# Up rows of the PEER stage: DVE adds them one rank at a time for 128 tokens, in place of PE; low parts shared anew between DVE and POOL

## The chip, the cores and the metric

One Trainium2 chip, one core. The metric is the device time of one execution in microseconds (us), the median of the runs of a kernel. Engines: PE (TensorE, matrix products), DVE (VectorE), ACT (ScalarE), POOL (GpSimd), SP (SyncE, which issues most DMAs). SBUF is the on-chip memory, PSUM the banks that PE writes.

## The reference

A two-layer decoder trunk on 512 tokens of width 1024, fp32. Layer 0 is attention, layer 1 a gated MLP; after each comes `peer_layer`, which this change touches:

```
q  = (xb @ w_query)                  # 8 heads x 2 halves x 128
s1, i1 = top_k(scores half 0, 16);  s2, i2 = top_k(scores half 1, 16)
top, ci = top_k(s1 + s2 pairs, 16)   # 16 of 128 * 128 experts for each head
idx = e1 * 128 + e2;  g = softmax(top)
hid = gelu(einsum('td,thkd->thk', xb, expert_down[idx]))
y   = einsum('thk,thkd->td', g * hid, expert_up[idx])
```

So each token reads 8 heads x 16 = 128 ranks: 128 rows of `expert_down` and 128 of `expert_up`, 1024 fp32 (4 KB) each.

## The kernel before

**Two ways for two groups of tokens.** For 384 tokens (`TD`) the kernel goes through all 16384 experts densely: down stage (128 tiles) and up stage (128 tiles) multiply whole weight tiles with dense hidden values and gates. For the first 128 tokens (`G`) it fetches only the chosen rows by indirect DMA. The up half of this second way is what changes.

**Weight tiles.** A tile is 128x1024 fp32, 512 KB. SP loads it into a ring of 4 (`raw`, L208); ACT makes its high part (`split_hi`, L215); POOL or DVE subtracts to get the low part (`split_lo`, L221); PE multiplies (`columns_step`, L246): 8 chunks of 3 matmuls, high x high, high x low, low x high (L254 to L256), 384 columns. High and low parts have rings of 3, and both are made `AHEAD` = 2 tiles early. `on_dve` (L82) says whose the low part is: in the up stages, from tile 2 on, every odd tile is DVE's, the others POOL's.

**The up stage, one tile v.** Each engine has its own program order; semaphores tie them. DVE (L1447 on): low part of tile v+2 where it is DVE's; `gate_slice` (L1433), the product of hidden values and gates for the next group of 8 tiles; a wait for PE to finish tile v; the addition of its bank to the residual (L1462); `gated_lo` (L1439). ACT (L1114 on): the high part of tile v+2 as soon as PE has finished tile v-1, then `gated_hi` (L1065), which waits for `gate_slice` and which `gated_lo` waits for. POOL (L1169 on): the low part of tile v+2, then the gathers due at this tile. PE: waits for the bank (`added`), the low part, in a group's first tile also for each chunk's `gated_lo`.

**The fetched rows.** Rows land in a ring of 7 buffers (`ring`, `UP_ORDER`) of 128x1024. A gather before brings the 128 ranks of one token, a rank in each partition (`experts_t`, the transposed indices), in the order of `row_token`. PE adds four tokens at a time (`rows_up`, L1247): the stationary operand is 32 columns of the buffer `zeroed`, all zero but for one column that holds the token's 128 weights (`place_w` on ACT writes them); 8 matmuls of 512 columns in fp32 into the banks `acc`. There are 32 such groups (`QUAD_TILE`), after tiles 13, 16, 19, 22, 25, 29 and so on to 112. Then ACT copies `acc`, PE turns it in 8 transposes (L1279) and DVE adds it to the residual (L1457). The weights are `hid_g` (L1453), turned by PE (L1273). A gather waits until the group that frees its buffer is done (L1164).

Around it: SP loads the hidden values and gates of a group two groups ahead, waiting for `gated_lo`. L1304 is the row product of the down half on DVE, with a PSUM operand. L1379 and L1381 are parts of the routing, L813 belongs to attention.

Of the kernel before, what the change touches and what calls it, by code (L numbers as in the profile page):

```python
# [72 lines left out]
G = P  # L73
# [21 lines left out]
def build(nc, weight_tiles, down0, down1, up0, up1, x_t, gains, key_t, masks, consts, lam_in, ws_t, b_sp, out_t):  # L95
# [4 lines left out]
    with ExitStack() as ctx:  # L100
# [46 lines left out]
        def norm_sems(turn):  # L147
# [13 lines left out]
                "gate_made": 2 * UNITS, "gate_copied": 2 * UNITS, "dotted": P, "hid_g": 1, "w_made": 1, "w_turned": 1, "w_copied": 1,  # L161
                "z_cleared": 1, "z_ready": G // 16, "quads": G // 4, "acc_copied": 1, "acc_turned": 2, "rows_added": 2,
# [4 lines left out]
        def peer_sems(tag):  # L167
            s = Sems()
            s.keys_loaded, s.q_copied, s.scored, s.score_copied = (sem(tag + k) for k in ("_keys_loaded", "_q_copied", "_scored", "_score_copied"))
            s.dve, s.top_shifted, s.top_exp, s.routed = (sem(tag + k) for k in ("_dve", "_top_shifted", "_top_exp", "_routed"))  # L170
            s.turned, s.turn_copied, s.equals, s.g_scaled, s.experts = (
                sem(tag + k) for k in ("_turned", "_turn_copied", "_equals", "_g_scaled", "_experts"))
            s.gelu_done, s.onehots, s.gate_made, s.gate_copied = (sem(tag + k) for k in ("_gelu_done", "_onehots", "_gate_made", "_gate_copied"))
            s.dotted, s.hid_g, s.w_made, s.w_turned, s.w_copied, s.z_cleared, s.z_ready = (
                sem(tag + k) for k in ("_dotted", "_hid_g", "_w_made", "_w_turned", "_w_copied", "_z_cleared", "_z_ready"))
            s.quads, s.acc_copied, s.acc_turned, s.rows_added = (sem(tag + k) for k in ("_quads", "_acc_copied", "_acc_turned", "_rows_added"))
# [724 lines left out]
        experts_t = side[:, 1440:1568].bitcast(U32)  # L901
        experts = side[:, 1568:1696].bitcast(U32)
        w_t = side[:, 1568:1696]
# [4 lines left out]
        zeroed = side[:, 0:1088].rearrange("p (b z) -> p b z", b=2)  # L908
# [12 lines left out]
        acc = ps[:, 5:7, :]  # L921
# [24 lines left out]
        QUADS = G // 4  # L946
        DENSE = (0, 1, 7)
        QUAD_TILE = [13 + q * 32 // 10 for q in range(QUADS)]
        W_TILE = 3
# [3 lines left out]

        def quads_at(v):
            return [q for q in range(QUADS) if QUAD_TILE[q] == v]

        def row_token(j):

            return G // 4 * (j % 4) + j // 4
# [18 lines left out]
        GATHER_UP_AT += [PDOWN + QUAD_TILE[(j - UP_RING) // 4] + 1 + (j - UP_RING) % 4 // 2 for j in range(UP_RING, P)]  # L978
# [67 lines left out]
        def peer_act(act, layer):  # L1046
# [58 lines left out]
            def place_w(c):  # L1105

                if c < 2:
                    act.wait_ge(s.w_copied, was["w_copied"] + 1)
                else:
                    act.wait_ge(s.quads, was["quads"] + 4 * (c - 1))  # L1110
                dst = zeroed[:, c % 2, 31:543].rearrange("p (g i r) -> p g i r", g=4, i=4)[:, :, :, 0]
                act.copy(dst, w_t.rearrange("p (g m) -> p g m", g=4)[:, :, 4 * c:4 * c + 4]).then_inc(s.z_ready, 1)

            for v in range(PUP):  # L1114
                ahead_hi(act, n0 + PQ + PDOWN + v)
                if v == W_TILE:
                    act.wait_ge(s.dotted, was["dotted"] + P)
                    act.activation(hid_g, hid_g, ACT.Gelu_apprx_tanh).then_inc(s.hid_g, 1)
                if v == W_TILE + 4:
                    act.wait_ge(s.w_turned, was["w_turned"] + 1)  # L1120
                    act.copy(w_t, ps[:, 4, 0:P]).then_inc(s.w_copied, 1)
                    act.wait_ge(s.z_cleared, was["z_cleared"] + 1)
                    place_w(0)
                    place_w(1)
                for c in range(2, QUADS // 4):
                    if v == QUAD_TILE[4 * c] - 2:
                        place_w(c)
                if v == QUAD_TILE[-1] + 2:
                    act.wait_ge(s.quads, was["quads"] + QUADS)
                    act.copy(pair[:, :, :], acc).then_inc(s.acc_copied, 1)  # L1130
                if v // 8 + 1 < GROUPS:
                    gated_hi(v // 8 + 1, v % 8)
                elif layer == 0 and v % 8:
                    c = v % 8 - 1
                    if c % 4 == 0:
                        act.wait_ge(s.rows_added, c // 4 + 1)
                    act.wait_ge(s.added, PUP - DC + c + 1)
                    norm_square(act, sn, c)

        def peer_pool(pool, layer):  # L1140
# [14 lines left out]
            def gather_up(j):  # L1155

                if j == 0:
                    pool.wait_ge(s.turn_copied, was["turn_copied"] + 1)
# [22 lines left out]
        def peer_pe(pe, layer):  # L1181
# [46 lines left out]
            for h in range(PDOWN):  # L1228
# [18 lines left out]
            def rows_up(q):  # L1247

                c, i = q // 4, q % 4
                pe.wait_ge(s.z_ready, was["z_ready"] + c + 1)  # L1250
                for j in range(4 * q, 4 * q + 4):
                    pe.wait_ge(up_gathered[j % UP_RING], 16 * (layer * UP_COUNT[j % UP_RING] + j // UP_RING + 1))
                if q == 0:
                    for d in range(2):
                        pe.matmul(acc[:, d, :], zeroed[:, 1, 0:1].to_broadcast([P, P]), ring[6][:, d * 512:(d + 1) * 512],
                                  start=True, stop=False, skip_group_check=True)
                for d in range(2):
                    for g in range(4):
                        z0 = 32 * (4 * g + i) + 31 - q
                        last = pe.matmul(acc[32 * g:32 * g + 32, d, :], zeroed[:, c % 2, z0:z0 + 32],  # L1260
                                         ring[UP_ORDER[(4 * q + g) % UP_RING]][:, d * 512:(d + 1) * 512],
                                         start=False, stop=q == QUADS - 1, skip_group_check=True)
                last.then_inc(s.quads, 1)

            for v in range(PUP):
# [5 lines left out]
                if v == W_TILE + 3:  # L1271
                    pe.wait_ge(s.w_made, was["w_made"] + 1)
                    pe.transpose(ps[:, 4, 0:P], hid_g, ident).then_inc(s.w_turned, 1)  # L1273
                for q in quads_at(v):
                    rows_up(q)
                if v == QUAD_TILE[-1] + 3:
                    pe.wait_ge(s.acc_copied, was["acc_copied"] + 1)
                    for c in range(DC):
                        turn = pe.transpose(ps[:, (7, 4)[c // 4], c % 4 * P:(c % 4 + 1) * P], pair[:, c // 4, c % 4 * P:(c % 4 + 1) * P], ident)  # L1279
# [3 lines left out]
        def peer_dve(dve, layer):  # L1283
# [142 lines left out]
            dve.memset(side[:, 0:1088], 0.0).then_inc(s.z_cleared, 1)  # L1426
# [20 lines left out]
            for v in range(PUP):  # L1447
# [321 lines left out]
```

## Time and profile before

| | us |
|---|---|
| median of 3 runs | 3310.04 (3305.21 to 3313.45) |
| the profiled execution | 3305.32 |
| its span, first to last instruction | 3303.6 |
| PE busy | 3242.8 (98%) |
| DVE busy | 1739.7 (53%) |
| ACT busy | 1392.5 (42%) |
| POOL busy | 1866.1 (56%) |

The span is that of the profiled execution between its first and last instruction. Matmuls are pipelined, so a busy PE need not be at its peak. DMA was 243 GB/s in the mean. The up stage of layer 0 lies at about 1071 to 1672 us, that of layer 1 at about 2699 to 3301. Timeline rows: start (us from the span's start), length (us), engine, line, operation, output<-inputs, count, and in brackets the idle time before it and what ended it.

### The profile page before, as it was taken

The numbers are of one execution on the slowest core, as the hardware profiler recorded it, in microseconds if no ns is written. First come the engines' busy times: TensorE is split into PE (matmuls) and PEld (weight loads), VectorE is DVE, ScalarE is ACT, GpSimd is POOL, SyncE is SP. The second block draws the span as 40 slices with busy tenths as digits, with TensorE's granted clock in tenths as the row PEclk, the third lists the DMA queues.
The fourth block names the chain that finished last, engine by engine and source line by source line (L and its number), as shares of the span: only waits on it lengthen the run. The fifth ranks groups of instructions, "written<-read, shape, count | busy, mean of one in ns | idle before, by whom it ended". The sixth has DMA issues, their size and how long they took to land.

```text
span 3303.6 us, 48436 instructions
## 1 busy us (share of the span) xinstructions
PE 3242.8 (98%) x18888; PEld 2979.3 (90%) x18888; DVE 1739.7 (53%) x3840; ACT 1392.5 (42%) x2521; POOL 1866.1 (56%) x1079
## 2 busy tenths in 40 slices
PE   7998999999999999999999999999999999999999
PEld 6766899999999988888988878999999999888889
DVE  5254167996773444444432311789867634444443
ACT  4354233338884333333333332333488743333332
POOL 4323358986656355555354653689865564555552
PEclk9998999999999999999999999999999999999999
DMA  3211237888999688888532222489899987888883
GB/s 118 83 33 34 94 121 280 309 317 304 335 335 357 244 327 335 333 325 322 198 109 96 77 102 79 148 313 323 299 330 330 332 337 267 319 330 331 334 330 121
DMA packets 260227, 801.98 MB, mean 243 GB/s; under 512 B 23968, under 2 KB 73120, under 8 KB 259488
## 3 DMA queue, kind: packets, MB, share of 16 engines
q1 hardware_dynamic: 186272, 530.41, 44.5%
q0 software_dynamic: 73728, 268.47, 21.5%
q8 instruction: 151, 2.47, 0.3%
q14 instruction: 76, 0.62, 0.1%
HBM read 699.17 MB, written 99.61 MB: 242 GB/s over the span
## 4 chain that ended last, share of the span: by engine, by line
PE 82%; DVE 12%; issue 2%; POOL 1%; ACT 1%; DMA 1%; DVEq 0%; POOLq 0%; ACTq 0%
PE banks L254 21%; PE banks L256 21%; PE banks L255 21%; PE banks L1224 5%; PE banks L1260 4%; DVE arena L1304 2%; PE banks L269 1%; PE banks L270 1%; PE banks L271 1%; DVE arena L1379 1%; DVE gathered_rows L1304 1%; PE banks L1192 1%; PE banks L602 1%; DVE arena L1383 1%; DVE side L1321 1%
## 5 line engine op out<-in xcount | busy, mean ns | idle before, releaser
L221 POOL TENSOR_TENSOR weights_lo<-raw_ring,weights_hi 128x1024 fp32r<-128x1024 f32 x498 | 1247.9, 2507 | 1118.7 <-ACT weights_hi L215 1116.6
L254 PE MATMUL banks<-operand_hi,weights_hi 128*128 128x384 f32 (+1 forms) x4648 | 1604.0, 345 | 2.0 <-ACT arena L1100 1.2
L256 PE MATMUL banks<-operand_hi,weights_lo 128*128 128x384 f32 (+1 forms) x4648 | 1584.0, 341 | 0.0
L255 PE MATMUL banks<-operand_lo,weights_hi 128*128 128x384 f32 (+1 forms) x4648 | 1583.8, 341 | 0.0
L254 PEld LDWEIGHTS banks<-operand_hi,weights_hi 128*128 128x128 f32 x4648 | 872.9, 188 | 78.9 <-issue 54.3
L215 ACT CAST weights_hi<-raw_ring 128x1024 fp32r<-128x1024 f32 x624 | 653.4, 1047 | 641.2 <-PE banks L256 563.5
L255 PEld LDWEIGHTS banks<-operand_lo,weights_hi 128*128 128x128 f32 x4648 | 873.0, 188 | 21.4 <-issue 1.4
L256 PEld LDWEIGHTS banks<-operand_hi,weights_lo 128*128 128x128 f32 x4648 | 872.4, 188 | 21.7
L1462 DVE TENSOR_TENSOR residual<-residual,banks 128x384 f32<-128x384 f32 x256 | 141.9, 554 | 666.4 <-PE banks L256 666.4
L1100 ACT ACTIVATE arena<-banks 128x384 f32<-128x384 f32 x256 | 126.1, 493 | 540.3 <-PE banks L256 532.6
L1065 ACT CAST operand_hi<-arena 128x384 fp32r<-128x384 f32 x256 | 130.8, 514 | 267.7 <-DVE arena L1433 267.7
L1071 ACT ACTIVATE arena<-operand_hi,side 128x128 f32<-128x128 f32 x768 | 235.4, 394 | 0.0
L1166 POOL DMA_INDIRECT arena<-up,side x146 | 154.2, 1057 | 73.7 <-PE banks L1260 40.5
L1421 DVE TENSOR_TENSOR operand_hi<-banks,side 128x1024 fp32r<-128x1024 f32 x96 | 117.5, 1224 | 147.5 <-PE banks L1224 147.4
L1224 PE MATMUL banks<-arena,operand_hi 128*128 128x128 f32 x1536 | 188.1, 276 | 1.6 <-ACT arena L1082 1.6
L1224 PEld LDWEIGHTS banks<-arena,operand_hi 128*128 128x128 f32 x1536 | 183.6, 192 | 4.3 <-issue 4.1
L1433 DVE TENSOR_TENSOR arena<-arena 128x384 f32<-128x384 f32 x256 | 149.2, 587 | 40.1 <-DMA arena<-gate_scratch 40.1
L1304 DVE CUSTOM_DVE_ANT_0 arena<-arena,banks 128x1024 f32<-128x1024 f32 x126 | 152.2, 1216 | 25.1 <-DMA arena<-down,side 23.4
L221 DVE TENSOR_TENSOR weights_lo<-raw_ring,weights_hi 128x1024 fp32r<-128x1024 f32 x126 | 154.4, 1226 | 10.6 <-ACT weights_hi L215 3.2
L1439 DVE TENSOR_TENSOR operand_lo<-arena,operand_hi 128x384 fp32r<-128x384 f32 x256 | 142.7, 560 | 15.3 <-ACT operand_hi L1065 15.3
L1152 POOL DMA_INDIRECT arena<-down,side x126 | 130.9, 1039 | 24.6 <-issue 11.3
L1260 PE MATMUL banks<-arena,side 128*32 128x512 f32 x584 | 122.6, 598 | 0.0
(210 smaller groups left out, 2902.3 us busy)
## 6 DMA issues: line engine op xcount, KB each, us to landing
raw_ring<-weight_tiles SPq DMA_DIRECT2D x624, 512.0 KB, 4.2
gate_scratch<-arena SPq DMA_DIRECT2D x24, 2048.0 KB, 14.4
arena<-gate_scratch SPq DMA_DIRECT2D x128, 384.0 KB, 7.6
hid_scratch<-arena SPq DMA_DIRECT2D x60, 768.0 KB, 7.3
arena<-hid_scratch SPq DMA_DIRECT2D x120, 384.0 KB, 5.9
arena<-up,side POOLq DMA_INDIRECT x146, 7.4
residual<-x_t SPq DMA_DIRECT2D x2, 1024.0 KB, 6.5
arena<-key_t SPq DMA_DIRECT2D x2, 1024.0 KB, 4.8
```

Source lines behind the costliest of these rows:

```text
L215: act.copy(wh[:, n % WRING, :], raw[:, n % RING, :]).then_inc(hi_split, 1)
L221: eng.tensor_tensor(wl[:, b, :], raw[:, n % RING, :], wh[:, b, :].bitcast(F32), ALU.subtract).then_inc(done, 1)
L254: pe.matmul(out, w_hi, x_hi[:, c, :], start=start and c == 0, stop=False)
L255: pe.matmul(out, w_hi, x_lo[:, c, :], start=False, stop=False)
L256: last = pe.matmul(out, w_lo, x_hi[:, c, :], start=False, stop=stop and c == DC - 1)
L1071: last = act.mul(oh2[:, u % 2, t, :], eq2[:, u % 2, t, :].bitcast(F32), columns_t[:, 2, 8 * u + t:8 * u + t + 1])
L1166: pool.indirect_dma_start(ring[UP_ORDER[j % UP_RING]], None, up_rows[layer], bass.IndirectOffsetOnAxis(ap=experts_t[:, t:t + 1], axis=0)). ...
L1224: last = pe.matmul(out[:, t, :], oh1[:, b, tk, :].bitcast(F32), oh2[:, b, tk, :], start=t == 0, stop=True, skip_group_check=True)
L1260: last = pe.matmul(acc[32 * g:32 * g + 32, d, :], zeroed[:, c % 2, z0:z0 + 32], ring[UP_ORDER[(4 * q + g) % UP_RING]][:, d * 512:(d + 1) * ...
L1304: dve.tensor_tensor_reduce(out=row, in0=row, in1=x_rows, scale=1.0, scalar=0.0, op0=ALU.mult, op1=ALU.add, accum_out=hid_g[:, k:k + 1]).th ...
L1433: dve.tensor_tensor(hid_in[b][:, j, :].rearrange("p (n t) -> p n t", n=GATE_BLOCKS), hid_in[b][:, j, :].rearrange("p (n t) -> p n t", n=GA ...
L1439: dve.tensor_tensor(up_lo[g % 2][:, j, :], hid_in[1 - g % 2][:, j, :], up_hi[g % 2][:, j, :].bitcast(F32), ALU.subtract).then_inc(s.gated_ ...
```

## The change

The gather now brings, for rank j, one row for each of the 128 tokens, token t in partition t; the untransposed `experts` give the indices. DVE multiplies the row buffer by the weight of its token (column r of `hid_g`, a scalar for each partition) and adds to `acc`, which now lies in SBUF (`side[:, 0:1024]`). There are 128 ranks, one to a tile from tile 2 to tile 115 (`RANK_TILE`), two in 14 tiles (2, 10, 18, ... 50, 59, 67, ... 107). In DVE's order a rank stands behind the low part and ahead of `gate_slice`. PE's groups, the zeroed buffer, `place_w`, the turning of weights and indices, ACT's copy of `acc` are gone; PE turns `acc` after tile 116. The product with the gates that gives the weights comes at tile 1 instead of 4. A gather waits for the one rank that frees its buffer and is issued one tile after it. `on_dve` gives DVE every fourth low part (v % 4 == 1), POOL the others.

```diff
-        if 2 <= v < PUP and v % 2 == 1:
+        if 2 <= v < PUP and v % 4 == 1:
...
-        QUAD_TILE = [13 + q * 32 // 10 for q in range(QUADS)]
-        W_TILE = 3
+        RANK_TILE = [2 + k * 114 // P for k in range(P)]
+        LAST_RANK = RANK_TILE[-1]
...
-        GATHER_UP_AT += [PDOWN + QUAD_TILE[(j - UP_RING) // 4] + 1 + (j - UP_RING) % 4 // 2 for j in range(UP_RING, P)]
+        GATHER_UP_AT += [PDOWN + RANK_TILE[j - UP_RING] + 1 for j in range(UP_RING, P)]
...
                 if j >= UP_RING:
-                    pool.wait_ge(s.quads, was["quads"] + (j - UP_RING) // 4 + 1)
-                t = row_token(j)
+                    pool.wait_ge(s.weighted, was["weighted"] + j - UP_RING + 1)
                 pool.indirect_dma_start(ring[UP_ORDER[j % UP_RING]], None, up_rows[layer],
-                                        bass.IndirectOffsetOnAxis(ap=experts_t[:, t:t + 1], axis=0)).then_inc(up_gathered[j % UP_RING], 16)
+                                        bass.IndirectOffsetOnAxis(ap=experts[:, j:j + 1], axis=0)).then_inc(up_gathered[j % UP_RING], 16)
...
-                for q in quads_at(v):
-                    rows_up(q)
-                if v == QUAD_TILE[-1] + 3:
-                    pe.wait_ge(s.acc_copied, was["acc_copied"] + 1)
+                if v == LAST_RANK + 1:
+                    pe.wait_ge(s.weighted, was["weighted"] + P)
...
-            dve.memset(side[:, 0:1088], 0.0).then_inc(s.z_cleared, 1)
+            dve.wait_ge(s.onehots, was["onehots"] + UNITS)
+
+            def add_row(r):
+
+                row = ring[UP_ORDER[r % UP_RING]]
+                dve.wait_ge(up_gathered[r % UP_RING], 16 * (layer * UP_COUNT[r % UP_RING] + r // UP_RING + 1))
+                if r == 0:
+                    dve.wait_ge(s.w_made, was["w_made"] + 1)
+                    dve.tensor_scalar(acc, row, hid_g[:, 0:1], None, ALU.mult).then_inc(s.weighted, 1)
+                else:
+                    dve.wait_ge(s.weighted, was["weighted"] + r)
+                    dve.scalar_tensor_tensor(out=acc, in0=row, scalar=hid_g[:, r:r + 1], in1=acc, op0=ALU.mult, op1=ALU.add).then_inc(s.weighted, 1)
...
+                for r in range(P):
+                    if RANK_TILE[r] == v:
+                        add_row(r)
```

## Rows read from the trace of the kernel before

**Rows 1.** The page's chain that ended last, shares by line.
```profile
PE banks L254 21%; PE banks L256 21%; PE banks L255 21%; PE banks L1224 5%; PE banks L1260 4%; DVE arena L1304 2%; PE banks L269 1%; PE banks L270 1%; PE banks L271 1%; DVE arena L1379 1%; DVE gathered_rows L1304 1%; PE banks L1192 1%; PE banks L602 1%; DVE arena L1383 1%; DVE side L1321 1%
```

**Rows 2.** Timeline, DVE, 1160:1183 us; start, length, line, operation, [idle before].
```profile
1167.71 1.23 DVE L221 TENSOR_TENSOR weights_lo<-raw_ring,weights_hi 128x1024 fp32r<-128x1024 f32 x1
1168.86 0.55 DVE L1433 TENSOR_TENSOR arena<-arena 128x384 f32<-128x384 f32 x1
1170.79 0.55 DVE L1462 TENSOR_TENSOR residual<-residual,banks 128x384 f32<-128x384 f32 x1 [1.38 <-PE banks L256]
1171.26 0.55 DVE L1439 TENSOR_TENSOR operand_lo<-arena,operand_hi 128x384 fp32r<-128x384 f32 x1
1171.72 0.55 DVE L1433 TENSOR_TENSOR arena<-arena 128x384 f32<-128x384 f32 x1
1174.95 0.55 DVE L1462 TENSOR_TENSOR residual<-residual,banks 128x384 f32<-128x384 f32 x1 [2.67 <-PE banks L256]
...
1181.16 0.56 DVE L1462 TENSOR_TENSOR residual<-residual,banks 128x384 f32<-128x384 f32 x1 [3.44 <-PE banks L256]
```

**Rows 3.** Busy time of each engine, first to last row group, layer 0.
```profile
1131.28:1606.99 475.71, 475.71 (x2876) 423.44 (x2880) 206.26 (x343) 154.59 (x203) 258.33 (x171) 1.00 0.85 322
```

**Rows 4.** DMA of that stretch: 40 slices, then totals.
```profile
GB/s 254 257 344 345 259 378 317 310 323 410 250 348 392 275 322 347 346 258 402 285 307 332 403 227 376 400 276 273 379 345 276 391 291 309 296 411 243 388 378 136
DMA packets 45397, 153.05 MB, mean 322 GB/s; under 512 B 5041, under 2 KB 5041, under 8 KB 45366
...
q0 software_dynamic: 17424, 63.45, 34.8%
```

**Rows 5.** Lines L1255 and L1260: ns min/median/max, first and last start us.
```profile
L1255 PE MATMUL banks<-arena,side x8: 592/592/592, 1129.4 to 2758.9; 128*128 128x512 f32 x8
...
L1260 PE MATMUL banks<-arena,side x584: 592/592/618, 1131.2 to 3236.5; 128*32 128x512 f32 x195
```

**Rows 6.** DVE groups of L813 in 225:310 us; last: busy us, mean ns.
```profile
L813 DVE SCALAR_TENSOR_TENSOR arena<-arena,small 128x384 f32<-128x384 f32 x4 | 2.5, 619 | 0.1
...
L813 DVE SCALAR_TENSOR_TENSOR arena<-pair,small,arena 128x256 f32<-128x256 f32 x3 | 1.5, 485 | 0.1
...
L813 DVE SCALAR_TENSOR_TENSOR arena<-arena,small 128x128 f32<-128x128 f32 x3 | 1.1, 352 | 0.1
```

**Rows 7.** Timeline, all engines, 484:488 us.
```profile
484.03 4.55 POOL L221 TENSOR_TENSOR weights_lo<-raw_ring,weights_hi 128x1024 fp32r<-128x1024 f32 x1 [1.76 <-ACT weights_hi L215]
484.04 2.29 DVE L1379 TENSOR_TENSOR arena<-side 128x2048 bf16<-128x2048 bf16 x1
...
486.36 3.30 DVE L1381 TENSOR_TENSOR arena<-arena,side 128x2048 bf16<-128x2048 bf16 x1
```

**Rows 8.** Timelines of POOL and of DVE, 2199:2202 us.
```profile
2199.64 2.40 POOL L221 TENSOR_TENSOR weights_lo<-raw_ring,weights_hi 128x1024 fp32r<-128x1024 f32 x1 [0.65 <-ACT weights_hi L215]
...
2199.16 0.29 DVE L1371 SCALAR_TENSOR_TENSOR side<-side 128x128 f32<-128x128 f32 x1
...
2199.74 2.45 DVE L1374 SCALAR_TENSOR_TENSOR side<-side 128x128 f32<-128x128 f32 x1
```

**Rows 9.** Lines L1433, L1304: ns min/median/max.
```profile
L1433 DVE TENSOR_TENSOR arena<-arena x256: 545/552/2756, 1050.8 to 3265.4; 128x384 f32<-128x384 f32 x128
...
L1304 DVE CUSTOM_DVE_ANT_0 arena<-arena,banks x126: 1209/1217/1223, 542.6 to 2647.1; 128x1024 f32<-128x1024 f32 x126
```

**Rows 10.** Timeline, POOL, 1161:1175 us.
```profile
1168.04 1.71 POOL L1166 DMA_INDIRECT arena<-up,side  x1 [0.31 <-issue]
1171.92 2.62 POOL L221 TENSOR_TENSOR weights_lo<-raw_ring,weights_hi 128x1024 fp32r<-128x1024 f32 x1 [2.17 <-ACT weights_hi L215]
```

**Rows 11.** Timeline, ACT, 1168:1175 us.
```profile
1170.78 1.05 ACT L215 CAST weights_hi<-raw_ring 128x1024 fp32r<-128x1024 f32 x1 [0.83 <-PE banks L256]
1172.31 0.51 ACT L1065 CAST operand_hi<-arena 128x384 fp32r<-128x384 f32 x1 [0.47 <-DVE arena L1433]
```

**Rows 12.** Line L1166, the up gathers: us from issue to landing.
```profile
DMA to landing us min/median/max: 4.5/7.3/12.2
```

More of the change, by code:

```diff
@@ L160, in build @@
                 "turned": 1, "turn_copied": 1, "equals": UNITS, "g_scaled": UNITS, "experts": 1, "gelu_done": PDOWN, "onehots": UNITS,
-                "gate_made": 2 * UNITS, "gate_copied": 2 * UNITS, "dotted": P, "hid_g": 1, "w_made": 1, "w_turned": 1, "w_copied": 1,
-                "z_cleared": 1, "z_ready": G // 16, "quads": G // 4, "acc_copied": 1, "acc_turned": 2, "rows_added": 2,
+                "gate_made": 2 * UNITS, "gate_copied": 2 * UNITS, "dotted": P, "hid_g": 1, "w_made": 1,
+                "weighted": P, "acc_turned": 2, "rows_added": 2,
                 "gated": PUP, "gated_hi": PUP, "gated_lo": PUP, "added": PUP,
@@ L173, in peer_sems @@
             s.gelu_done, s.onehots, s.gate_made, s.gate_copied = (sem(tag + k) for k in ("_gelu_done", "_onehots", "_gate_made", "_gate_copied"))
-            s.dotted, s.hid_g, s.w_made, s.w_turned, s.w_copied, s.z_cleared, s.z_ready = (
-                sem(tag + k) for k in ("_dotted", "_hid_g", "_w_made", "_w_turned", "_w_copied", "_z_cleared", "_z_ready"))
-            s.quads, s.acc_copied, s.acc_turned, s.rows_added = (sem(tag + k) for k in ("_quads", "_acc_copied", "_acc_turned", "_rows_added"))
+            s.dotted, s.hid_g, s.w_made, s.weighted, s.acc_turned, s.rows_added = (
+                sem(tag + k) for k in ("_dotted", "_hid_g", "_w_made", "_weighted", "_acc_turned", "_rows_added"))
             s.hid_stored = [sem(f"{tag}_hid_stored{b}") for b in range(2)]
@@ L900, in build @@
         experts_f = side[:, 1440:1568]
-        experts_t = side[:, 1440:1568].bitcast(U32)
         experts = side[:, 1568:1696].bitcast(U32)
-        w_t = side[:, 1568:1696]
         hid_g = side[:, 1696:1824]
@@ L907, in build @@
         columns_t = side[:, 0:3 * TD].rearrange("p (q t) -> p q t", q=3)
-        zeroed = side[:, 0:1088].rearrange("p (b z) -> p b z", b=2)
+        acc = side[:, 0:TILE]
         oph_flat, opl_flat = (a.rearrange("p b c t -> p (b c t)") for a in (oph, opl))
@@ L920, in build @@
         x_rows = ps[:, 5:7, :].rearrange("p b t -> p (b t)")
-        acc = ps[:, 5:7, :]
         iota8 = ps[:, 4, 0:KEYS][:, None, :].to_broadcast([P, 8, KEYS])
@@ L945, in build @@
         ROUTE_DOTS, UNIT_DOTS, TAIL_DOTS = 60, 60, 8
-        QUADS = G // 4
         DENSE = (0, 1, 7)
-        QUAD_TILE = [13 + q * 32 // 10 for q in range(QUADS)]
-        W_TILE = 3
+        RANK_TILE = [2 + k * 114 // P for k in range(P)]
+        LAST_RANK = RANK_TILE[-1]
         def units_at(h):
             return [u for u in range(UNITS) if UNIT_TILE[u] == h]
[L954 to L959, printed above, removed]
         def dot_tile(k):
@@ L1103, in peer_act @@
                         gated_hi(0, j)
[L1105 to L1112, printed above, removed]
             for v in range(PUP):
                 ahead_hi(act, n0 + PQ + PDOWN + v)
-                if v == W_TILE:
+                if v == 0:
                     act.wait_ge(s.dotted, was["dotted"] + P)
                     act.activation(hid_g, hid_g, ACT.Gelu_apprx_tanh).then_inc(s.hid_g, 1)
[L1119 to L1130, printed above, removed]
                 if v // 8 + 1 < GROUPS:
@@ L1157, in gather_up @@
                 if j == 0:
-                    pool.wait_ge(s.turn_copied, was["turn_copied"] + 1)
                     for half in range(2):
@@ L1237, in peer_pe @@
                         for tt in range(1, TT):
-                            pe.transpose(ps[:, 2 + q, (tt - 1) * P:tt * P], src[:, tt, :], ident)
-                    pe.transpose(ps[:, 4, TD:T], experts_f, ident).then_inc(s.turned, 1)
+                            last = pe.transpose(ps[:, 2 + q, (tt - 1) * P:tt * P], src[:, tt, :], ident)
+                    last.then_inc(s.turned, 1)
                 for u in units_at(h):
@@ L1245, in peer_pe @@
             pe.wait_ge(s.gate_copied, was["gate_copied"] + 2 * UNITS)
[L1247 to L1263, printed above, removed]
             for v in range(PUP):
@@ L1270, in peer_pe @@
                              ready=(lambda c, g=g: pe.wait_ge(s.gated_lo, was["gated_lo"] + 8 * g + c + 1)) if v % 8 == 0 else None)
-                if v == W_TILE + 3:
-                    pe.wait_ge(s.w_made, was["w_made"] + 1)
-                    pe.transpose(ps[:, 4, 0:P], hid_g, ident).then_inc(s.w_turned, 1)
-                for q in quads_at(v):
-                    rows_up(q)
-                if v == QUAD_TILE[-1] + 3:
-                    pe.wait_ge(s.acc_copied, was["acc_copied"] + 1)
+                if v == LAST_RANK + 1:
+                    pe.wait_ge(s.weighted, was["weighted"] + P)
                     for c in range(DC):
-                        turn = pe.transpose(ps[:, (7, 4)[c // 4], c % 4 * P:(c % 4 + 1) * P], pair[:, c // 4, c % 4 * P:(c % 4 + 1) * P], ident)
+                        turn = pe.transpose(ps[:, (7, 4)[c // 4], c % 4 * P:(c % 4 + 1) * P], acc[:, c * P:(c + 1) * P], ident)
                         if c % 4 == 3:
@@ L1412, in peer_dve @@
             for q in range(3):
-                dve.tensor_copy(columns_t[:, q, :], ps[:, 2 + q, 0:TD])
-            dve.tensor_copy(experts_t, ps[:, 4, TD:T]).then_inc(s.turn_copied, 1)
+                last = dve.tensor_copy(columns_t[:, q, :], ps[:, 2 + q, 0:TD])
+            last.then_inc(s.turn_copied, 1)
             dve.wait_ge(s.turn_copied, was["turn_copied"] + 1)
@@ L1450, in peer_dve @@
                     split_lo(dve, u0 + v + AHEAD, lo_dve)
-                if v == W_TILE + 1:
+                if v == 1:
                     dve.wait_ge(s.hid_g, was["hid_g"] + 1)
                     dve.tensor_tensor(hid_g, hid_g, g_own, ALU.mult).then_inc(s.w_made, 1)
-                if v == QUAD_TILE[-1] + 5:
+                for r in range(P):
+                    if RANK_TILE[r] == v:
+                        add_row(r)
+                if v == LAST_RANK + 3:
                     for half in range(2):
```

## The prediction

> **What bounds the kernel now.** I read the chain of waits first. By line it is nearly all TensorE (PE): the three matmul lines of the weight products hold 63% of the span, and L1260, the matmuls that add the fetched up rows, another 4% [rows 1]. In the up stage (128 weight tiles in each of two layers) the VectorE (DVE) timeline shows the pace. L1462 adds a finished tile to the residual, so its starts mark the ends of PE tiles: 1170.79 to 1174.95 is 4.16 us, a plain tile; 1174.95 to 1181.16 is 6.21 us, a tile with one group of L1260 (2.05 more) [rows 2]. PE is busy all 475.7 us of the stretch from first to last group, DVE 206, ScalarE (ACT) 155 and GpSimd (POOL) 258, with the clock at 1.00 (2.4 GHz) [rows 3]. So the up stage is PE-bound, and what leaves PE leaves the time if nothing else rises above 4.16 us a tile. DMA moves 153 MB in it [rows 4].
>
> **What the change takes off PE.** Per layer 32 groups x 2.05 = 65.6 us, the four clearing matmuls of L1255 (from 1129.4 to the first L1260 at 1131.2, 1.8 us) and a transpose of 0.1 us [rows 5]: 67.5, over two layers 135. The eight closing transposes stay. The memset, the ACT copies that place weights and the turning of the expert indices also go; they lie on engines with idle time, and I count them as nothing (an error under 1 us).
>
> **What it adds.** DVE gets 128 multiply-adds of 128x1024 per layer (the first a plain multiply), in tiles 2 to 115, one a tile and two in 14 of them. POOL gets 31 more weight low parts per layer, in each fourth tile's place DVE keeps one (29 of the 114 tiles with rows; in the other 85 POOL makes it).
>
> Length of one multiply-add. The trace has scalar_tensor_tensor with two SBUF tensors undisturbed only up to 384 columns: 352, 485 and 619 ns at 128, 256 and 384 columns, a steady 134 ns per 128 [rows 6]. That gives 352 + 7 x 133.5 = 1.29 us at 1024; the 128x1024 subtraction of L221 took 1.23 on DVE [rows 2]. I take 1.29, bounds 1.22 and 1.40.
>
> By busy time alone this fits. DVE per tile: three 0.55 operations, started 0.47 apart, 1.12 rows of 1.2 and a quarter of 1.23: about 3.1 us of 4.16 [rows 2]. POOL: three quarters of 2.62 and 1.12 gathers started 1.25 apart: 3.4 [rows 10]. DMA: the software queue (q0, the gathers) moved 63.45 of 153.05 MB, so the rest moved 89.6 for the stretch's 99 tiles, 0.905 a tile; a gather is 128 rows of 4 KB, 0.52 MB, times 1.12 is 0.59. One tile then needs 1.49 MB, 358 GB/s at 4.16 us, where slices of that stretch reached 400 to 412 [rows 4]. That is near the limit, but it doesn't bind at the pace I come to below.
>
> **DVE and POOL exclude each other.** This decides. At 484.03 a POOL low part began together with a DVE operation on two SBUF tensors (L1379, 2.29 us); it took 4.55 instead of 2.40, ending 2.25 after L1379. The next DVE operation, L1381, was issued at 486.36, back to back, yet POOL had gone in between: L1381 took 3.30 and ended 1.08 after POOL [rows 7]. The same holds for scalar_tensor_tensor: L1374, normally 0.29 us, started 0.10 after a POOL low part and took 2.45, ending 0.15 after it [rows 8]. And L1433, 0.55 us in the median, has a maximum of 2.76 [rows 9]. DVE operations with a PSUM operand run beside POOL: L1304 has no spread at all over 126 instructions (1.21 to 1.22 us) in the down stages, where POOL makes every low part [rows 9]. So: two-SBUF operations of DVE and POOL's low parts don't overlap; whoever is in finishes, and a POOL operation that waits goes in before DVE's next one. The Trainium skill, "SBUF — State Buffer", section "SBUF: two separate sides", says the same: the port pair that both share is locked for a whole instruction and the loser blocks fully. By that rule, the trace agrees.
>
> The kernel before lives with it: POOL's low part starts at 1171.92, DVE's product ends at 1172.27, POOL ends at 1174.54, 2.27 later [rows 2, 10], and DVE has no two-SBUF work until the next tile. A row addition fills just that hole. The new cycle, counted from the end of one gate product (L1433) in a tile whose successor's low part falls to POOL:
> - 0.04 ACT starts L1065 (DVE end 1172.27, ACT 1172.31), ends 0.55 [rows 2, 11]; ACT then makes the next high part (L215, 1.05), from about 0.47 to 1.52.
> - DVE's L1462 needs PSUM only and is beside this; L1439 waits for L1065: 0.58 to 1.13.
> - DVE's row addition starts 0.09 before that end (as 1171.26 to 1171.72), 1.04 to 2.33.
> - POOL starts 0.09 after the high part (1171.83, 1171.92), at 1.61, in the middle of the row, gets in at 2.33 and ends 2.27 later, 4.60.
> - The gate product, issued at 2.25, ends 0.41 after POOL (0.55 less the 0.14 that L1374 and L1381 show): 5.0.
>
> So such a tile takes 5.0 us, above PE's 4.16. Where DVE makes the low part, L221 starts when the high part is there, 1.55, the row starts 1.15 later (1167.71 to 1168.86), 2.70 to 3.98, and the product ends at 4.45. A second row in a tile adds 1.2.
>
> The waits that this adds: DVE's wait for a gathered row stands ahead of gate product, residual addition and low part, and through them PE; but a gather lands in 7.3 us (longest 12.2) [rows 12] and is issued about five tiles, 24 us, before its use. POOL's gathers wait for a row added one tile earlier. PE waits for the low part: it comes at 4.60 of a cycle, two tiles ahead, and PE then idles 0.3 to 0.8 us a tile. At each group's first tile PE also waits for the last L1439 of the group before, which ends some 6 us later than the tile could begin its last chunk; that tile ends 3 us late, still ahead of DVE, which comes to it only in the cycle after, and the tiles behind make it good out of their idle 0.8.
>
> **The sum per layer.** 85 x 5.0 = 425; 29 x 4.45 = 129; 14 second rows x 1.2 = 17: 571 us between the low part of tile 3 and that of tile 117. Ahead of it two tiles, less what is left of one, 8.0; behind it 11 tiles of 4.16, 45.8. Together 625. Before: 128 x 4.16 = 532.5, with 67.5 and 0.9 for the closing transposes 601. The stage grows by 24 us, two layers by 47. The profiled execution is 3305.3 us (span 3303.6); it lies 4.7 below the median of 3310.0. 3305.3 + 47 = 3352, on the median 3357. I predict 3356. Its own range: rows of 1.22 to 1.40 move it by -17 to +28 (256 rows), a handoff 0.1 us shorter or longer in each of 228 cycles by 23 either way: 3330 to 3384.
>
> A second rule of the skill speaks against the change more strongly: "Vector Engine (DVE) Microarchitecture Reference", section "7. Points that are easy to get wrong", says that scalar_tensor_tensor with two non-bf16 SBUF sources runs at half throughput. As a rival below it is priced from rows; the slope of 134 ns per 128 columns, about that of L221 (1.23 us for 1024), speaks against it here.
>
> **Rivals.**
> - PE stays the bound, because POOL and DVE slip past each other. Every tile 4.16: 3310 - 135 = 3175. For it: DVE and POOL have the time on paper. Against it: exclusive work alone is row 1.3, L1439 and L1433 1.1, POOL 2.3: 4.7 in a POOL tile [rows 2, 10].
> - POOL settles late. If its low part becomes ready after the gate product has begun (from 2.25 of the cycle on, 0.64 later than I reckon; a gather held by a DVE operation, as the 1.71 us one at 1168.04, can push it [rows 10]), L1462 and L1065 hide beside it. From POOL's end, L1439 ends 0.41 later, the row 1.20 after that, the product 0.47 after the row, and POOL's next 2.27 after the product: 4.35. Stage 370 + 129 + 17 + 54 = 570, 31 less: 3247, faster. Against it: next time the high part is long ready, POOL comes right after its gather, inside the row again, and is back in the slow order.
> - The two orders alternate. Half of the POOL tiles at 4.35: 598 per layer, about 3303 on the median, no change.
> - Half throughput of the multiply-add: each row twice 133.5 x 8, 1.07 us longer, 256 rows: 274 more, 3630.
>
> **Chances.** Forecast 0.72, PE bound 0.07, POOL late 0.11, alternating 0.08, half throughput 0.02. A measurement of this kernel tells some 0.3%, 10 us, from no change. Faster 0.07 + 0.11 = 0.18; same 0.08; slower 0.74. The range goes down to the late order, 3235, and up to the end of the forecast's own, 3384; left out are PE bound, half throughput and a little of each edge.
>
> **What would show it.** Right: L1260 gone; L1462 starts about 5.0 us apart in tiles 3 to 115, 4.4 in each fourth; gate products (L1433) of 2.7 us or so in three tiles of four; POOL's low part 3.0 us instead of 2.62; PE idle on POOL's weights_lo; DMA share no higher than 0.85. The row additions 1.29 each. Wrong: L1462 at 4.16 apart (PE bound), at 4.35 with L1439 stretched rather than L1433 (late order), or DVE idle on up rows.

## The result, and the profile after

| | before | after |
|---|---|---|
| median, runs on the same chip | 3311.74 us (4 runs) | 3360.97 us (4 runs, 3359.51 to 3362.71) |
| ratio | | 1.0154, 95% interval 1.0138 to 1.0170 |
| profiled execution, span | 3305.32, 3303.6 | 3361.27, 3359.5 |
| up stage, first to last addition to the residual | 597.0 in either layer | 622.5 in either layer |

The change makes the kernel 1.5% slower. In the changed kernel the low part is L220, the row addition L1379, the gate product L1386, the residual addition L1418, `gated_lo` L1392, `gated_hi` L1053, the high part L214, the weight products L253 to L255, the up gather L1131.

The chain of waits by engine, which answers to [rows 1] (there PE held 82%):

```profile
PE 49%; DVE 35%; issue 8%; ACT 5%; POOL 2%; DMA 1%; DVEq 0%; ACTq 0%; POOLq 0%
```

The same stretch of time as in [rows 3]; columns: window, its length, busy us of PE, PEld, DVE, ACT, POOL, granted clock, DMA share, GB/s:

```profile
1131.28:1606.99 475.71, 418.56 (x2270) 402.38 (x2269) 453.90 (x416) 139.29 (x190) 328.51 (x178) 0.97 0.84 301
```

DVE went from 206 to 454 us of 475.7, PE from 476 to 419. DMA moved 301 GB/s instead of 322: it is not what binds. The granted clock is 0.97 in the mean here, because it falls briefly to its lower level (1.2 GHz) nine times in this up stage, eight of them around the first tile of a group, where PE waits for L1392 (up to 2.0 us). The tiles during and right after such a fall take 4.98 to 5.07 us, as long as the others, so the clock does not set the pace.

DVE's timeline, two successive cycles, to be read beside [rows 2]. A cycle runs from the end of one gate product to the end of the next. In the first POOL makes the low part; in the second DVE does (L220 at 1308.66):

```profile
1299.39 2.73 DVE L1386 TENSOR_TENSOR arena<-arena 128x384 f32<-128x384 f32 x1
1302.05 0.54 DVE L1418 TENSOR_TENSOR residual<-residual,banks 128x384 f32<-128x384 f32 x1
1302.70 0.56 DVE L1392 TENSOR_TENSOR operand_lo<-arena,operand_hi 128x384 fp32r<-128x384 f32 x1
1303.18 1.28 DVE L1379 SCALAR_TENSOR_TENSOR side<-gathered_rows,side 128x1024 f32<-128x1024 f32 x1
1304.37 2.76 DVE L1386 TENSOR_TENSOR arena<-arena 128x384 f32<-128x384 f32 x1
1307.06 0.54 DVE L1418 TENSOR_TENSOR residual<-residual,banks 128x384 f32<-128x384 f32 x1
...
1308.66 1.23 DVE L220 TENSOR_TENSOR weights_lo<-raw_ring,weights_hi 128x1024 fp32r<-128x1024 f32 x1 [0.39 <-ACT weights_hi L214]
1309.81 1.28 DVE L1379 SCALAR_TENSOR_TENSOR side<-arena,side 128x1024 f32<-128x1024 f32 x1
1311.00 0.55 DVE L1386 TENSOR_TENSOR arena<-arena 128x384 f32<-128x384 f32 x1
1311.47 0.55 DVE L1418 TENSOR_TENSOR residual<-residual,banks 128x384 f32<-128x384 f32 x1
```

POOL and ACT in the first of the two cycles, answering to [rows 10, 11]:

```profile
1303.70 3.01 POOL L220 TENSOR_TENSOR weights_lo<-raw_ring,weights_hi 128x1024 fp32r<-128x1024 f32 x1 [0.76 <-ACT weights_hi L214]
1306.87 1.09 POOL L1131 DMA_INDIRECT arena<-up,side  x1 [0.15 <-issue]
```

```profile
1302.16 0.51 ACT L1053 CAST operand_hi<-arena 128x384 fp32r<-128x384 f32 x1 [3.52 <-DVE arena L1386]
1302.58 1.05 ACT L214 CAST weights_hi<-raw_ring 128x1024 fp32r<-128x1024 f32 x1
```

Count from 1302.12, where L1386 (1299.39, 2.73 long) ends. ACT starts L1053 0.04 later, the next high part from 0.46 to 1.51. DVE's L1392 starts at 0.58, the row at 1.06 and ends at 2.34. POOL starts at 1.58, in the middle of the row, and ends at 4.59, 2.25 after it. L1386, issued at 2.25 and 0.55 us of work, ends at 5.01, 0.42 after POOL. That is the whole cycle. In the second there is no low part on POOL, L1386 takes 0.55, and the cycle is 4.42 (1307.13 to 1311.55).

The lines over all their runs (ns min/median/max), beside [rows 9]; the low parts are those of the stretch 1131 to 1607 us:

```profile
L1386 DVE TENSOR_TENSOR arena<-arena x256: 544/2730/2765, 1053.5 to 3323.2; 128x384 f32<-128x384 f32 x128
```

```profile
L1379 DVE SCALAR_TENSOR_TENSOR side<-arena,side x144: 1275/1279/3233, 1090.4 to 3300.7; 128x1024 f32<-128x1024 f32 x144
```

```profile
L220 POOL TENSOR_TENSOR weights_lo<-raw_ring,weights_hi x72: 2532/2999/3024, 1133.7 to 1605.0; 128x1024 fp32r<-128x1024 f32 x72
L220 DVE TENSOR_TENSOR weights_lo<-raw_ring,weights_hi x23: 1224/1225/1226, 1148.7 to 1590.5; 128x1024 fp32r<-128x1024 f32 x23
```

The product went from 0.55 to 2.73 us in the median, without having more work; POOL's low part from 2.62 to 3.00. Who waits for whom in the first up stage (us in total, times, longest):

```profile
ACT operand_hi L1053 <- DVE arena L1386: 406.5, 116, 4.7
...
PE banks L253 <- POOL weights_lo L220: 28.6, 31, 2.2
PE banks L253 <- DVE operand_lo L1392: 28.3, 14, 2.0
DVE residual L1418 <- PE banks L255: 27.4, 9, 3.6
```

ACT waits 406 us for the product in this one up stage; before it was 134 us in the same stage (L1065 for L1433). PE's waits are for POOL's low parts and for L1392. No DVE row addition waited for a gather.

### The profile page after: what moved, and what is told of

Its sections match the earlier page's. It is cut to its first block, busy times and chain, and to the rows that moved or that the text cites. A ratio compares the mean times of both kernels' runs of the same rounds, so it can differ in the third digit from the quotient of the medians.

```text
span 3359.5 us, 46724 instructions
## 1 busy us (share of the span) xinstructions
PE 3170.4 (94%) x17852; PEld 2981.0 (89%) x17852; DVE 2344.3 (70%) x4028; ACT 1364.5 (41%) x2501; POOL 2104.0 (63%) x1143
## 4 chain that ended last, share of the span: by engine, by line
PE 49%; DVE 35%; issue 8%; ACT 5%; POOL 2%; DMA 1%; DVEq 0%; ACTq 0%; POOLq 0%
DVE arena L1386 13%; PE banks L253 11%; PE banks L254 11%; PE banks L255 11%; DVE side L1379 10%; PE banks L1189 5%; ACT operand_hi L1053 3%; ACT weights_hi L214 2%; DVE arena L1246 2%; PE banks L268 1%; PE banks L269 1%; PE banks L270 1%; DVE gathered_rows L1246 1%; DVE arena L1321 1%; POOL weights_lo L220 1%
## 5 line engine op out<-in xcount | busy, mean ns | idle before, releaser
L220 POOL TENSOR_TENSOR weights_lo<-raw_ring,weights_hi 128x1024 fp32r<-128x1024 f32 x562 | 1471.8, 2620 | 1007.8 <-ACT weights_hi L214 1005.2
L253 PE MATMUL banks<-operand_hi,weights_hi 128*128 128x384 f32 (+1 forms) x4648 | 1619.9, 349 | 129.6 <-POOL weights_lo L220 58.2
L255 PE MATMUL banks<-operand_hi,weights_lo 128*128 128x384 f32 (+1 forms) x4648 | 1597.2, 344 | 0.0
L253 PEld LDWEIGHTS banks<-operand_hi,weights_hi 128*128 128x128 f32 x4648 | 882.7, 190 | 187.7 <-issue 97.2
L255 PEld LDWEIGHTS banks<-operand_hi,weights_lo 128*128 128x128 f32 x4648 | 882.3, 190 | 21.8
L254 PEld LDWEIGHTS banks<-operand_lo,weights_hi 128*128 128x128 f32 x4648 | 882.5, 190 | 21.4 <-issue 1.4
L214 ACT CAST weights_hi<-raw_ring 128x1024 fp32r<-128x1024 f32 x624 | 652.2, 1046 | 157.7 <-PE banks L255 82.5
L1386 DVE TENSOR_TENSOR arena<-arena 128x384 f32<-128x384 f32 x256 | 497.9, 1949 | 41.3 <-DMA arena<-gate_scratch 41.3
L1053 ACT CAST operand_hi<-arena 128x384 fp32r<-128x384 f32 x256 | 130.6, 513 | 827.5 <-DVE arena L1386 811.8
L1379 DVE SCALAR_TENSOR_TENSOR side<-arena,side 128x1024 f32<-128x1024 f32 x144 | 200.2, 1390 | 1.7
L1418 DVE TENSOR_TENSOR residual<-residual,banks 128x384 f32<-128x384 f32 x256 | 139.1, 543 | 62.1 <-PE banks L255 62.1
L1131 POOL DMA_INDIRECT arena<-up,side x146 | 163.5, 1120 | 28.8 <-issue 20.1
L1392 DVE TENSOR_TENSOR operand_lo<-arena,operand_hi 128x384 fp32r<-128x384 f32 x256 | 145.4, 571 | 47.2 <-ACT operand_hi L1053 23.1
L1230 DVE COPY arena<-banks 128x512 f32<-128x512 f32 x32 | 22.2, 692 | 180.1 <-PE banks L1157 180.1
```

Of the source, the lines that this page charges most:

```text
L214: act.copy(wh[:, n % WRING, :], raw[:, n % RING, :]).then_inc(hi_split, 1)
L220: eng.tensor_tensor(wl[:, b, :], raw[:, n % RING, :], wh[:, b, :].bitcast(F32), ALU.subtract).then_inc(done, 1)
L253: pe.matmul(out, w_hi, x_hi[:, c, :], start=start and c == 0, stop=False)
L254: pe.matmul(out, w_hi, x_lo[:, c, :], start=False, stop=False)
L255: last = pe.matmul(out, w_lo, x_hi[:, c, :], start=False, stop=stop and c == DC - 1)
L1053: act.copy(up_hi[g % 2][:, j, :], hid_in[1 - g % 2][:, j, :]).then_inc(s.gated_hi, 1)
```

## The experiments

All times are medians; each ratio is against runs of the kernel before on the same chip.

**1. The new share alone.** The kernel before, one line changed.

```diff
-        if 2 <= v < PUP and v % 2 == 1:
+        if 2 <= v < PUP and v % 4 == 1:
```

> The kernel before with the new share alone: DVE makes every fourth weight low part, POOL the others, and PE still adds the rows. Exclusion theory: DVE has no two-SBUF work between the gate product and the end of the tile, so POOL's low part collides with nothing long; PE stays the bound, 3311 us within 10. Rival (POOL's added load makes the loss: 31 more low parts of 2.6 us per layer): 3330 to 3360.

Measured: 3308.73 us against 3309.60, ratio 0.9997 (0.9981 to 1.0013). No change. The stretch of [rows 3] in this kernel:

```profile
1131.28:1606.99 475.71, 475.71 (x2868) 422.48 (x2867) 178.34 (x322) 155.17 (x203) 316.89 (x196) 1.00 0.87 323
```

POOL's busy time rose from 258 to 317 us of 475.7 and PE stayed full. More low parts on POOL cost nothing by themselves. The rival (3330 to 3360) is out.

**2. The rows alone, with the old share.** The changed kernel with `v % 2 == 1`.

> The changed kernel with the old share (DVE every second low part), so DVE is the busier. Exclusion theory: 57 tiles of 5.00 and 57 of 4.41 us instead of 85 and 29, 16.5 us less per layer: 3361 - 33 = 3328. Rival (DVE is simply overloaded, each low part on it costs 1.15 us): 28 more per layer, 3361 + 64 = 3425.

Measured: 3327.88 us, ratio 1.0059 (1.0038 to 1.0080). The forecast was 3328. DVE now makes 28 low parts more per layer than in the changed kernel (1.23 us each), and the whole is 33 us faster. In its trace tiles of 5.00 and 4.42 us alternate.

**3. No low part on POOL in the up stage, from tile 2 on.** The changed kernel with the condition `2 <= v < PUP` and nothing else.

> The changed kernel with every low part of the up stages from tile 2 on made by DVE and none by POOL. Exclusion theory: no tile has a collision, each takes 4.41 us: 85 x 0.59 = 50 us less per layer, 3361 - 100 = 3261, faster than both kernels though DVE has the most work. Rival (DVE overloaded by busy time): 85 x 1.15 more per layer, 3361 + 195 = 3556.

Measured: 3269.97 us (3264 to 3287), ratio 0.9890 (0.9853 to 0.9927). Its groups (busy us, mean ns, idle before):

```profile
L220 POOL TENSOR_TENSOR weights_lo<-raw_ring,weights_hi 128x1024 fp32r<-128x1024 f32 x372 | 908.8, 2444 | 659.2 <-ACT weights_hi L214 656.8 <-issue 0.3
...
L220 DVE TENSOR_TENSOR weights_lo<-raw_ring,weights_hi 128x1024 fp32r<-128x1024 f32 x252 | 308.9, 1226 | 98.0 <-ACT weights_hi L214 97.5
...
L1386 DVE TENSOR_TENSOR arena<-arena 128x384 f32<-128x384 f32 x256 | 148.7, 585 | 41.6 <-DMA arena<-gate_scratch 41.6
```

With the most work of all variants on DVE, 126 more low parts of 1.23 us than the kernel before has, the kernel is 91 us faster than the changed one and 40 faster than before. The gate product is back at 0.59 us in the mean. Tiles take 4.42 us, 5.81 with two rows. The rival, that busy time on DVE sets the pace, is out by some 290 us. But the tiles are not back at PE's 4.16: with no low part of POOL left to collide with, DVE's own order, with its product behind low part and row and ACT waiting for the product (368 us in the first up stage), still costs 0.26 us a tile, as the 4.41 of the forecast has it. The kernel is 9 us above the forecast; in the profiled execution, which took 3266.4, the up stages are 577.9 and 575.1 us where 622.5 - 50 = 572.5 was expected.

**4. The gate product ahead of the row.** Sum still in SBUF.

```diff
+                if g + 1 < GROUPS:
+                    gate_slice(g + 1, k)
                 for r in range(P):
                     if RANK_TILE[r] == v:
                         add_row(r)
...
-                if g + 1 < GROUPS:
-                    gate_slice(g + 1, k)
                 dve.wait_ge(tiles_done, u0 + v + 1)
```

> The changed kernel with one swap in DVE's order: the gate product ahead of the row, the sum still in SBUF. Exclusion theory: the product no longer waits behind row and low part, so ACT's chain starts earlier; but row, product, L1439 and POOL's low part still exclude each other. Counted by the same steps: a POOL tile 4.85 us, a DVE tile 3.8: 85 x 4.85 + 29 x 3.8 + 17 + 54 = 593 a layer against 625, 3361 - 64 = 3297 (3285 to 3325). Rival (only DVE's position ahead of ACT matters, no exclusion): 3176 to 3190.

Measured: 3298.89 us, ratio 0.9972 (0.9961 to 0.9982). Most POOL tiles take 4.8 us, DVE tiles 3.73. DVE and then POOL in one stretch of it (line numbers as for the changed kernel, the product at L1386, the row at L1379):

```profile
1299.14 0.54 DVE L1392 TENSOR_TENSOR operand_lo<-arena,operand_hi 128x384 fp32r<-128x384 f32 x1
1299.61 0.55 DVE L1386 TENSOR_TENSOR arena<-arena 128x384 f32<-128x384 f32 x1
1300.08 3.43 DVE L1379 SCALAR_TENSOR_TENSOR side<-arena,side 128x1024 f32<-128x1024 f32 x1
1303.43 0.54 DVE L1418 TENSOR_TENSOR residual<-residual,banks 128x384 f32<-128x384 f32 x1
1303.90 3.30 DVE L1392 TENSOR_TENSOR operand_lo<-arena,operand_hi 128x384 fp32r<-128x384 f32 x1
1307.12 0.55 DVE L1386 TENSOR_TENSOR arena<-arena 128x384 f32<-128x384 f32 x1
```

```profile
1299.13 3.29 POOL L220 TENSOR_TENSOR weights_lo<-raw_ring,weights_hi 128x1024 fp32r<-128x1024 f32 x1 [2.90 <-ACT weights_hi L214]
1302.58 1.75 POOL L1131 DMA_INDIRECT arena<-up,side  x1 [0.16 <-issue]
1304.36 2.41 POOL L220 TENSOR_TENSOR weights_lo<-raw_ring,weights_hi 128x1024 fp32r<-128x1024 f32 x1
```

DVE and POOL still exclude each other, only other operations pay: the row is issued at 1300.08 and takes 3.43 instead of 1.28, L1392 takes 3.30 instead of 0.55. The rows also show an exception to the order that the prediction assumed. POOL's low part was issued at 1299.13 and had to wait for L1392 (1299.14), and yet the product, issued at 1299.61, went in ahead of it and kept its 0.55; POOL ended 2.26 us after the product. The changed order wins 62 us on the changed kernel and 9 on the one before.

**5. The sum in PSUM, old order.** A row addition then reads one tensor from SBUF and one from PSUM (banks 5 and 6, `x_rows`, free in the up stage).

```diff
-        acc = side[:, 0:TILE]
+        acc_rows = side[:, 0:TILE]
...
+        acc = x_rows
...
+                if v == LAST_RANK + 1:
+                    act.wait_ge(s.weighted, was["weighted"] + P)
+                    act.copy(acc_rows, acc).then_inc(s.acc_copied, 1)
...
-                if v == LAST_RANK + 1:
-                    pe.wait_ge(s.weighted, was["weighted"] + P)
+                if v == LAST_RANK + 2:
+                    pe.wait_ge(s.acc_copied, was["acc_copied"] + 1)
```

> The changed kernel with the sum in PSUM, but in the old order (row ahead of the gate product). Exclusion theory: POOL no longer waits for the row, starts its low part 1.61 us after the last product and ends at 4.01; the product, issued at 2.25, waits for it and ends at 4.42. 85 x 4.42 + 29 x 4.45 + 8 + 54 = 567 a layer, 58 less than 625: 3361 - 116 = 3245. Rival (the row costs by its length alone): 3361 again.

Measured: 3252.19 us, ratio 0.9828 (0.9811 to 0.9844); 7 us above the forecast. The up stages explain it: 568.6 us each from first to last residual addition, where 622.5 - 58 = 564.5 was expected. The row addition is the same instruction with the same 1.28 us, and only where the sum lies is different. DVE (row L1383, product L1390, residual L1422), then POOL:

```profile
1302.78 1.28 DVE L1383 SCALAR_TENSOR_TENSOR banks<-gathered_rows,side,banks 128x1024 f32<-128x1024 f32 x1
1303.98 2.15 DVE L1390 TENSOR_TENSOR arena<-arena 128x384 f32<-128x384 f32 x1
1306.05 0.54 DVE L1422 TENSOR_TENSOR residual<-residual,banks 128x384 f32<-128x384 f32 x1
```

```profile
1303.31 2.39 POOL L220 TENSOR_TENSOR weights_lo<-raw_ring,weights_hi 128x1024 fp32r<-128x1024 f32 x1 [2.43 <-ACT weights_hi L214]
```

POOL starts in the middle of the row, as in the changed kernel, but takes 2.39 us and not 3.01: the row no longer holds it. The product, which has two SBUF tensors, still waits: 2.15 us, ending 0.43 after POOL. Nor does POOL hold the row: the 254 row additions with the sum in PSUM take 1.28 to 1.29 us, where the longest in the changed kernel took 3.23.

**6. The sum in PSUM and the product first.** Edits 4 and 5 together.

> The changed kernel with the sum of the rows in two PSUM banks instead of SBUF (ACT copies it to SBUF at the end), so that a row addition reads only one SBUF tensor, and with the gate product ahead of the row. Exclusion theory: the row runs beside POOL's low part, the product is done before POOL starts; nothing above 4.16 us a tile, PE-bound: 3311 - 135 = 3176, at most 10 more. Rival 1 (the length of DVE's work, not the exclusion, set the pace): 3340 to 3361. Rival 2 (DMA becomes the bound at 358 GB/s): 3200 to 3250, with DVE idle on up rows or ACT on weight tiles.

Measured: 3201.66 us, but from 3190.9 to 3224.0 over four runs, ratio 0.9692 (0.9648 to 0.9736). That is much faster than either kernel and 25 above what I expected, with an unusual spread. The windows of the first up stage up to tile 58 and from there (columns as above):

```profile
1084.00:1318.00 234.00, 234.00 (x1352) 234.00 (x1351) 177.43 (x246) 87.79 (x112) 170.46 (x105) 1.00 0.95 359
1318.00:1560.00 242.00, 235.99 (x1347) 234.46 (x1346) 237.33 (x244) 82.70 (x111) 175.12 (x102) 0.99 0.90 340
```

In the first window PE is full and the tiles take 4.16 us; in the second DVE is busy 237 of 242 us and PE is no longer full. DVE and POOL at the border:

```profile
1319.91 1.23 DVE L220 TENSOR_TENSOR weights_lo<-raw_ring,weights_hi 128x1024 fp32r<-128x1024 f32 x1
1321.05 0.55 DVE L1390 TENSOR_TENSOR arena<-arena 128x384 f32<-128x384 f32 x1
1321.53 1.28 DVE L1383 SCALAR_TENSOR_TENSOR banks<-gathered_rows,side,banks 128x1024 f32<-128x1024 f32 x1
1322.91 1.29 DVE L1383 SCALAR_TENSOR_TENSOR banks<-arena,side,banks 128x1024 f32<-128x1024 f32 x1
1324.11 0.55 DVE L1422 TENSOR_TENSOR residual<-residual,banks 128x384 f32<-128x384 f32 x1
1324.57 2.35 DVE L1396 TENSOR_TENSOR operand_lo<-arena,operand_hi 128x384 fp32r<-128x384 f32 x1
...
1329.44 2.75 DVE L1390 TENSOR_TENSOR arena<-arena 128x384 f32<-128x384 f32 x1
```

```profile
1324.12 2.39 POOL L220 TENSOR_TENSOR weights_lo<-raw_ring,weights_hi 128x1024 fp32r<-128x1024 f32 x1 [3.35 <-ACT weights_hi L214]
...
1329.02 2.77 POOL L220 TENSOR_TENSOR weights_lo<-raw_ring,weights_hi 128x1024 fp32r<-128x1024 f32 x1
```

Tile 59 is the first with two rows and a low part on DVE as well: from 1319.91 on 1.23 + 0.55 + 1.28 + 1.29 us and the two short ones, more than a tile. DVE arrives late at L1396 (1324.57), when POOL has begun its low part (1324.12), and waits for it; in the next tile the product waits (2.75 at 1329.44). Tiles of 4.8 us follow, but the first two times the delay costs nothing: DVE is at most 2.6 us late, and two short cycles (2.59 and 3.52 us, then 2.60 and 3.52) bring it back to PE's pace by tiles 65 and 73. Only after the third such tile, 75, does it meet POOL again and again before it has caught up (tiles 80 to 82 at 4.8 each), and from there the stage loses its 9 us against run 7. What decides whether DVE catches up was not tested.

**7. Two rows never where DVE has a low part.**

```diff
-        RANK_TILE = [2 + k * 114 // P for k in range(P)]
+        RANK_TILE = sorted(list(range(2, 116)) + list(range(2, 107, 8)))
```

> The kernel with the sum in PSUM and the product first, and the 14 tiles with two rows always tiles whose low part POOL makes (v % 8 == 2), never one with a low part on DVE. In the kernel without this the pace held 4.16 us up to tile 59, the first with two rows and a low part on DVE (5.3 us of work), and was 4.8 in many tiles after it. Theory (that pile-up pushes DVE late, and then product and L1439 fall behind POOL's low part): 4.16 in every tile, 5 us less per layer, 3180 to 3190. Rival (something later in the stage, DMA for one): the same 4.8 us tiles again, 3200.

Measured: 3175.32 us (3171.0 to 3177.5), ratio 0.9591 (0.9575 to 0.9607). Tiles are 4.16 us throughout, but for the one with the closing transposes (5.06), and the up stage takes 529.2 us in each layer. The same two windows:

```profile
1084.00:1318.00 234.00, 234.00 (x1352) 234.00 (x1351) 178.06 (x249) 88.34 (x114) 169.92 (x105) 1.00 0.95 358
1318.00:1560.00 242.00, 242.00 (x1398) 242.00 (x1397) 183.85 (x254) 92.08 (x118) 169.54 (x103) 1.00 0.91 347
```

And one cycle, DVE then POOL (L1383 is the row, L1396 `gated_lo`):

```profile
1300.71 0.55 DVE L1390 TENSOR_TENSOR arena<-arena 128x384 f32<-128x384 f32 x1
1301.18 1.28 DVE L1383 SCALAR_TENSOR_TENSOR banks<-arena,side,banks 128x1024 f32<-128x1024 f32 x1
...
1304.40 0.55 DVE L1396 TENSOR_TENSOR operand_lo<-arena,operand_hi 128x384 fp32r<-128x384 f32 x1
```

```profile
1300.90 2.62 POOL L220 TENSOR_TENSOR weights_lo<-raw_ring,weights_hi 128x1024 fp32r<-128x1024 f32 x1 [0.44 <-ACT weights_hi L214]
```

The row runs from 1301.18 to 1302.46 while POOL's low part runs from 1300.90 to 1303.52; after the row DVE is free until PE's tile ends. This version is 133 us faster than the kernel before and 186 faster than the changed one. The DMA share is 0.95 at 358 GB/s in its first window, with PE still full, so the demand that the prediction worked out per tile can be served.

## Why the prediction was right

**The step that decided** was the exclusion of DVE operations on two SBUF tensors and POOL's low parts, together with the order in which they take turns. It was read from the trace before [rows 7, 8] and holds in the changed kernel to a few hundredths: POOL's end behind the row's was put at 2.27 and was 2.25, the product's behind POOL's at 0.41 and was 0.42. Four runs separate it from load. The changed kernel, with less work on DVE and more on POOL, is slower than run 2. POOL's greater load alone costs nothing (run 1). With more work on DVE and none on POOL (run 3) it is faster. The same row with its sum in PSUM (run 5) leaves POOL alone, and the kernel is 109 us faster. The Trainium skill's rule in "SBUF — State Buffer", section "SBUF: two separate sides", excludes a DVE operation with two SBUF inputs against a GpSimd operation that reads SBUF; the traces agree on both sides, with 3.01 us for POOL's low part beside the row in the changed kernel and 2.39 beside the same row with its sum in PSUM (run 5).

The second half of the rule, that a waiting POOL operation goes in before DVE's next one, has no exception in the trace of the changed kernel, but it is not general: 31 times in run 4 and 10 times in run 6 the product passed a low part that was already waiting.

**Sizes.** Cycle with POOL's low part 5.0 forecast, 5.01 measured; with DVE's 4.45 and 4.42. Row 1.29 and 1.28. A second row 1.2; measured 6.13 - 5.00 = 1.13 in a POOL tile and 5.80 - 4.42 = 1.38 in a DVE tile. The stage was to grow by 24 us and grew by 25.5; for both layers 47 and 51. The profiled spans differ by 56; the other 5 us lie outside the up stages, in parts that the edit leaves alone, and the medians, 49 apart, do not show them. The forecast of 3356 is 5 us low, and 4 of them are the stages. Two slips in the prediction moved nothing: the highest slice of [rows 4] is 411 GB/s and not 412, and the spreads that it names, added up, give 3316 to 3407 and not 3330 to 3384.

**The PE side.** Taking the row groups off PE is worth what was worked out, 135 us, once nothing else rises above 4.16 us: run 7 measures 133. It was the sum of the rival "PE stays the bound". The exclusion is not all that stands against that rival: run 3 has no low part of POOL to collide with and its tiles still take 4.42 us, and run 5, whose rows are free of POOL, has 4.4 with the old order. It took the free row, the product first and the double rows apart to get back to 4.16.

**What moved no time.** The new share alone changes nothing (run 1); only with the rows does it cost. Of the 49 us some 18 are the rows' under the old share (run 2), and the other 31 are what the new share adds once the rows are on DVE. DMA was weighed as near its limit and does not bind. No idle time of DVE before a row addition was ended by a gather.

**The rivals.** The late order, priced at 4.35 a tile, did not occur in the changed kernel; I had argued it would be left at once. What did occur in run 6 is a slow pattern of 4.8 us that DVE falls into when it is late, at first for a few tiles and later for longer. I had not foreseen it: my expectation of 3176, at most 10 more, missed the 3201.66, because it took the kernel for PE-bound wherever the mean load fits. Half throughput for the multiply-add is refuted: 128x1024 in 1.28 us, both tensors fp32 in SBUF, where [rows 6] gave 1.29, and no shorter with one of them in PSUM. The Trainium skill's remark on this in "Vector Engine (DVE) Microarchitecture Reference", section "7. Points that are easy to get wrong", does not hold for this instruction when it is read as the rival was priced, each row twice as long; the measurement decides.

**Left open.** Runs 3 and 6 vary by 23 and 33 us between executions. For run 6 the slow pattern is a possible reason, not a shown one: only one execution of each was profiled. Why DVE's product sometimes passes a waiting POOL operation is open too.

## What to carry to other kernels

Before giving DVE an operation on two SBUF tensors, look what POOL reads at that moment: busy times add up only for operations that exclude each other, and then they add up across both engines. Here, keeping one operand in PSUM took the operation out of this exclusion at no cost in length. In an engine's order, what others wait for should stand ahead of a long operation. Where the pace only just fits, keep the heavy tiles apart: each late tile can bring new collisions, and from the third one on run 6 no longer made the delay good.

## What the runs showed of the hardware that was not expected

- In run 4 a gather also held DVE. L1392 was issued at 1303.90 while a gather was in its last 0.43 us (1302.58, 1.75 long, itself held by the row until 1303.51); the low part that followed it at 1304.36 went in first, and L1392 took 3.30 us. The same happened 27 times in that run, always at 3.27 to 3.30, and in no other trace of this case. In the kernel before, L1433 beside a gather kept its 0.55 us [rows 2, 10].
- scalar_tensor_tensor takes the same 1.28 us for 128x1024 with its second tensor and its output in PSUM as with both in SBUF.
- In run 4 DVE's product passed a POOL low part that was already waiting 31 times, in run 6 10 times, in the other traces never. Each time the low part and `gated_lo` had been issued within 0.02 us of each other (1299.13 and 1299.14 in the rows of run 4). The low part then took 3.26 to 3.30 us. Run 4 has 122 such near ties and run 6 42, the other traces 4 at most, and most end the other way: at 1290.61 in run 4 both were issued together, POOL went in before the product, and the low part took 2.81 us.
